# A two-block network on one core: constants loaded behind the first inputs, the feed-forward's first weights split ahead of the last residual, and attention filled by one paced lane

## The chip, the core and the metric

The kernel runs on one core of a Trainium2 chip. The metric is the device time of one execution in microseconds (us), 3388.86 us as the median of three runs before the change. The core's engines each run their own program in order and meet only at semaphores: TensorE (PE, matmuls), VectorE (DVE), ScalarE (ACT), GpSimd (POOL) and SyncE (SP), whose program here issues all DMAs on one queue.

## What is computed

Everything is float32. A first block (a gated linear attention layer and a dilated attention layer, both with memory attention) is followed by a second block of two layers, l = 0 and l = 1. The second block is where most of the change lies. Cut to what matters:

```python
def mixer(hl, hc, ...):                      # 512 latent rows, 256 context rows
    pl, pc = split_projection(hl @ w_in), split_projection(hc @ w_in)
    ... hgrn2_scan forwards and backwards, 4 heads, chunks of 64 ...
    ... diff_softmax_attend: s = q k^T (two maps), p = softmax(s), w = p0 - lam * p1, o = w v
    ... fourier_mix ...
    yl = concat([hgrn, diff, fourier]) @ w_out        # and yc for l = 0

def swiglu(h, w_i, w_o):
    g, u = split(h @ w_i, 2)
    return (silu(g) * u) @ w_o

for l in range(2):
    yl, yc = mixer(...)
    xl = xl + ml[2] * rms_norm(yl, g[1])
    xl = xl + ml[5] * rms_norm(swiglu(adaln(xl, g[2], ml[3], ml[4]), w_ffn_in[l], w_ffn_out[l]), g[3])
    if l == 0: the same for xc
```

The rows are held as tiles of 128: six tiles (four latent, two context) in layer 0, four in layer 1. In the first block, `first_block` begins with `rmsnorm(mem, mem_norm_w)`, which is the first arithmetic of the whole kernel.

## The kernel before

The kernel records one plan: `P.add(kind, ...)` appends a step, and afterwards each engine's program goes through the steps in the order recorded and runs its own handler for each kind. So the order in which the Python code adds steps is the order of the instructions on every engine. No scheduler moves anything; a step that has to wait holds back everything behind it on its engine. Generators (`project`, `prepare`, `levels_early`, `residual_rows`) yield between groups of steps, and `rounds`, `with_some` and `together` decide how two such lanes are mixed: `rounds` takes one step of each in turn, `with_some(a, b, 1.5)` takes one of `a` and then 1.5 of `b`.

**Start.** The step `setup` makes SP issue the loads of `CONST_LOADS` (one of 68 KB and 16 small ones) and then the memory rows `in_mem` (1 MB). Three loads for the gates follow (`w_gate_up`, `k_gla` twice), then the first memory weights (1 MB) and `x`. PE's `setup` transposes the constants. ACT works out the memory rows' norm from a Square, then Ln and Exp; each function set needs a table (`ActQueue.activation` loads one, L169, when the function is not in the loaded set), and the Square is the first of them. All ACT functions have the line L171, and the first table load has it too.

**Attention stage.** `attention_stage` runs the differential attention, tile by tile and four heads per tile. For each head PE makes the scores (L2124), DVE the maxima (L2811) and the weights (L2818 to L2823), PE transposes the weights (L1919) and multiplies them with the values (L1915, 128x64). After a tile's last head DVE finishes with L2832, L2834, L2839. Between the pieces, `fill` takes steps from `filling`: the recurrence's projections `project(0)` and `project(1)`, and the preparation of the recurrence's first head, `prepare(heads[0])` (matmuls of 128x128, DVE L2616) and `levels_early(heads[0])`, the first unit's levels (DVE L2630 x7, one 1792-wide ACT exponential, DVE L2639 x7). What `filling` has left after the last head is recorded behind it, and then comes `fence()`, at which all engines meet. Behind the fence the recurrence begins.

**Output projection.** `project_out` multiplies tile by tile, halves c = 0 and c = 1 of the columns, with weights that were split into a high and a low part (OC0h and OC0l in layer 0, OC1h and OC1l in layer 1). Before a tile's products it records `turned(i + 1)`, the next tile's transposes, whose high part ACT or DVE writes to HI and whose low part DVE writes to LO (L2561). In the middle of each half `between` is called, and after each tile `after_y`. Both take a step of `rows`, which makes the gain rows: DVE L2771 and L2776 build a diagonal in AR, PE multiplies it with a block of ones (`rr`, MATMUL PS<-AR,CON), and ACT or DVE copies it out (L2781). The banks of `rr` are those of the transposes (0 and 1, ring `tr`). `after_y` then adds the residual `rs` (two ACT Squares of 512, DVE L2795, L2800, L2803) and the norm that begins the feed-forward (`norm_begin`: ACT Square, DVE L2482; `norm_end`: eight transposes of HNB, DVE L2494, L2498, and the low part L2504).

**Feed-forward.** Weights arrive by `stage_w` (1 MB each) and `convert` splits a quarter of them: ACT copies the high part to WC (`cvh`, 128x1024), then DVE subtracts to get the low part (`cvl`, L2856). The ring `wcr` has three pieces of WC, which lie over the parts OC. `up` multiplies a quarter (c of 0 to 3) for all tiles; the last tile's rows come later than the others', so the two opening quarters are multiplied first for the columns whose tiles are ready (512 in layer 0, 384 in layer 1), then `norm_end(last)` puts the last tile's transposes, and then the rest of the columns of both quarters (256 and 128 wide). `gated_ff` empties the banks of a block (ACT silu into EX, DVE L2862, ACT high part, DVE L2867), and `up` of the next block's c = 0 waits for all six banks together:

```python
need = [x for i in range(6) for x in ufree.get(i, ())] if c == 0 else []
up_n = up(c, o, [ready, *need], whole)
```

## Time and profile before

| | us |
|---|---|
| median of three runs | 3388.86 |
| lowest and highest | 3388.45, 3390.48 |
| profiled execution, its own time | 3390.33 |
| its span | 3389.0 |
| PE busy in the span | 3026.1 (89%) |
| DVE, ACT, POOL busy | 1578.2 (47%), 989.1 (29%), 325.3 (10%) |

The profile is of one execution. A row gives the start of a group of equal instructions, the time that they took, the engine, the line, the operation with output and input names, the number, and in brackets the idle time before them with what released the engine. PE runs at one of two clocks, 2.4 GHz where the granted clock is 1.00 and 1.2 GHz where it is 0.50; a window's value is the mean over the window.

### The profile page before, as it was taken

To read this page: it belongs to the slowest core of one execution; us is meant where nothing else is said; L and a number is where in the kernel's file an instruction comes from. 1 tells how busy PE (TensorE), PEld (TensorE's weight loads), DVE (VectorE), ACT (ScalarE), POOL (GpSimd) and SP (SyncE) were. 2 spreads that over 40 slices of the span, in tenths; PEclk is the share of its full clock that TensorE was granted. 3 is DMA by queue.
4 is the path that set the end of the run, shared out by engine and by line. 5 is a ranking of instruction groups with operands and counts; after the bars stand their busy time and mean duration, and the time that the engine had idled before them with its cause. 6 is when DMAs were issued, how large, how long until landed. Compare 5 with 4: busy or idle time off the path is not lost.

```text
span 3389.0 us, 44137 instructions
## 1 busy us (share of the span) xinstructions
PE 3026.1 (89%) x18434; PEld 2419.5 (71%) x18434; DVE 1578.2 (47%) x3075; ACT 989.1 (29%) x1913; POOL 325.3 (10%) x594
## 2 busy tenths in 40 slices
PE   6988899999989997887688999999999786789998
PEld 4657588888976566776466888887657676468886
DVE  3122534444442354768662433425535657644444
ACT  2011423232341344334232121212235333222222
POOL 0000000000000000555300000000100334100001
PEclk9999899999999997998798999999999788889999
DMA  5423232222221200323502121121020111123322
GB/s 175 156 97 113 90 111 57 56 57 64 61 107 74 69 13 1 97 76 106 175 18 70 50 75 63 50 75 63 38 62 13 29 28 37 50 71 104 99 87 75
DMA packets 227235, 246.62 MB, mean 73 GB/s; under 512 B 5488, under 2 KB 192988, under 8 KB 225500
## 3 DMA queue, kind: packets, MB, share of 16 engines
q1 hardware_dynamic: 227036, 243.79, 22.4%
q8 instruction: 146, 2.39, 0.3%
q14 instruction: 53, 0.43, 0.0%
HBM read 234.34 MB, written 9.44 MB: 72 GB/s over the span
## 4 chain that ended last, share of the span: by engine, by line
PE 52%; DVE 8%; issue 6%; ACT 3%; POOL 2%; DMA 1%; POOLq 0%; DVEq 0%; ACTq 0%; SPq 0%
PE PS L1915 49%; PE PS L1919 1%; ACT AR L171 1%; PE PS L2124 1%; DVE AR L2639 1%; POOL AR L2916 1%; DVE AR L2875 1%; DVE AR L2630 1%; POOL AR L2907 1%; DVE EX L2862 0%; ACT L169 0%; DVE AC L2867 0%; ACT EX L171 0%; ACT WC L171 0%; DMA WR<-in_w_in 0%
## 5 line engine op out<-in xcount | busy, mean ns | idle before, releaser
L1915 PE MATMUL PS<-HI,WC 128*128 128x512 f32 (+3 forms) x2144 | 581.8, 359 | 30.9 <-DVE EX L2862 12.5
L1915 PE MATMUL PS<-WR,HT 128*128 128x256 f32 (+2 forms) x2256 | 509.9, 384 | 13.3 <-ACT AR L171 7.1
L1915 PEld LDWEIGHTS PS<-WR,HT 128*128 128x128 f32 x2256 | 376.8, 197 | 122.1 <-issue 76.8
L1915 PEld LDWEIGHTS PS<-HI,WC 128*128 128x128 f32 x2144 | 389.7, 194 | 89.3 <-issue 13.1
L1915 PE MATMUL PS<-AR 128*64 128x64 f32 (+8 forms) x3756 | 330.2, 279 | 111.8 <-POOL AR L2916 34.7
L1915 PEld LDWEIGHTS PS<-AR 128*64 128x64 f32 (+5 forms) x3756 | 285.7, 182 | 164.3 <-issue 50.1
L1915 PE MATMUL PS<-LO,WC 128*128 128x512 f32 (+3 forms) x1072 | 384.3, 358 | 0.0
L171 ACT ACTIVATE AR<-PS 128x512 f32<-128x512 f32 (+4 forms) x383 | 164.5, 453 | 670.4 <-PE PS L1915 524.4
L1915 PE MATMUL PS<-HT,WR 128*128 128x256 f32 (+3 forms) x1136 | 348.9, 460 | 10.4 <-DMA WR<-in_w_in 4.6
L1915 PE MATMUL PS<-DW,DH 128*128 128x384 f32 (+1 forms) x1344 | 355.6, 347 | 1.0 <-ACT DH L171 1.0
L2856 DVE TENSOR_TENSOR WC<-WR,WC 128x1024 fp32r<-128x1024 f32 x132 | 161.6, 1225 | 390.6 <-ACT WC L171 390.6
L1915 PE MATMUL PS<-WC,AC 128*128 128x512 f32 x1320 | 318.2, 397 | 11.6 <-DVE AR L2875 9.9
L1915 PEld LDWEIGHTS PS<-WC,AC 128*128 128x128 f32 x1320 | 244.4, 189 | 80.1 <-DVE AR L2875 28.6
L1915 PEld LDWEIGHTS PS<-HT,WR 128*128 128x128 f32 (+2 forms) x1136 | 209.1, 190 | 117.7 <-issue 90.0
L171 ACT ACTIVATE WC<-WR 128x1024 fp32r<-128x1024 f32 x132 | 139.7, 1059 | 512.1 <-PE PS L1915 491.7
L1915 PEld LDWEIGHTS PS<-DW,DH 128*128 128x128 f32 x1344 | 240.8, 191 | 9.7 <-issue 7.1
L1915 PEld LDWEIGHTS PS<-LO,WC 128*128 128x128 f32 x1072 | 208.4, 194 | 27.7
L1915 PE MATMUL PS<-DW,DL 128*128 128x384 f32 (+1 forms) x672 | 226.5, 337 | 0.0
L1919 PE MATMUL PS<-CON,AR 128*128 128x128 f32 (+1 forms) x944 | 156.4, 294 | 71.9 <-ACT AR L171 18.5
L1919 PEld LDWEIGHTS PS<-CON,AR 128*128 128x128 f32 (+1 forms) x944 | 121.2, 151 | 112.8 <-issue 55.4
L171 ACT ACTIVATE EX<-PS 128x256 f32<-128x256 f32 (+2 forms) x158 | 67.6, 431 | 418.8 <-PE PS L1915 418.7
L2875 DVE TENSOR_TENSOR AR<-AR,PS 128x512 f32<-128x512 f32 x200 | 133.6, 682 | 46.1 <-PE PS L1915 46.1
(288 smaller groups left out, 3435.7 us busy)
## 6 DMA issues: line engine op xcount, KB each, us to landing
WR<-in_w_ffn_in SPq DMA_DIRECT2D x44, 1024.0 KB, 7.0
WR<-in_w_in_b SPq DMA_DIRECT2D x51, 512.0 KB, 5.9
WR<-in_w_mod SPq DMA_DIRECT2D x12, 2048.0 KB, 7.9
WR<-in_w_mod SPq DMA_DIRECT2D x24, 1024.0 KB, 5.4
WR<-in_w_ffn_out SPq DMA_DIRECT2D x22, 1024.0 KB, 4.9
WR<-in_w_in SPq DMA_DIRECT2D x40, 512.0 KB, 4.1
WR<-in_w_out SPq DMA_DIRECT2D x8, 2048.0 KB, 8.7
WR<-in_w_in_a SPq DMA_DIRECT2D x8, 1024.0 KB, 5.4
```

Of the source, the lines that this page charges most:

```text
L171: return self.o.activation(out, in_, func, **kw)
L1915: mm = lambda o, l, r, start, stop: e.o.matmul(o, l, r, start=start, stop=stop, skip_group_check=True)
L1919: m = e.o.transpose(bk[0:a.shape[1], 128 * i:128 * i + a.shape[0]], a, ident[0:a.shape[0], 0:a.shape[0]])
L2124: m = e.o.matmul(bank(2 * m_ + b)[:, 0:hi - lo], a.q[m_], a.k[m_][:, lo:hi], start=True, stop=True)
L2630: s = tt(v(x3[:, l, :])[:, :, 0 if rev else 1, :], b4[:, :, 0 if rev else 1, :], ref.broadcast_to([K, 128 // h, h]), ALU.subtract)
L2639: m = tt(v(x3[:, l, :]), v(x3[:, l, :]), v(H.q[:, 128 * i:128 * i + 256]), ALU.mult)
L2856: tt(lo, src, hi.bitcast(F32), ALU.subtract).then_inc(sem("cv_d"))
L2875: tt(y, y, bk, ALU.add).then_inc(sem("dn_d"))
L2907: s = tt(v(x3[:, l, :])[:, :, 1 if rev else 0, :], ref.broadcast_to([K, 128 // h, h]), b4[:, :, 1 if rev else 0, :], ALU.subtract)
L2916: m = tt(v(x3[:, l, :]), v(x3[:, l, :]), v(k[:, 128 * i:128 * i + 256]), ALU.mult)
```

## The change

Three places are rewritten.

At the start a step `begin` precedes everything: SP issues `in_mem` and the 68 KB constant, ACT loads the table of Ln and Exp. Then comes the first load of memory weights, then `setup` with the small constants, then `x`, and only then the three loads for the gates. PE and ACT still wait for all constants in `setup`.

In the output projection of both layers `after_y` no longer takes a step of `rows` at the first tile. For the last tile, the loads of the first feed-forward weights and the split of their first quarter are recorded ahead of `rs`, and each WC piece waits for the products that read the parts beneath it. The last tile's `norm_end` moves between the two opening quarters. `up` waits for each bank where it opens it, in the order 0, 2, 1, 3.

In the attention stage `filling` runs `project(0)`, then `project(1)` with 1.5 steps of preparation and first levels for each of its steps.

```diff
+    def preload(self, func):
...
-        P.add("setup")
+        P.add("begin")
...
         fetch()
+        P.add("setup")
         P.add("inputs")
+        P.add("ld", "gcon", WGU[0:16, :], A["w_gate_up"].rearrange("o a n -> (o a) n"), 0, ())
+        P.add("ld", "gcon", R64, A["k_gla"][:, 0:512].bitcast(F32), 0, ())
+        P.add("ld", "gcon", CAUSAL, A["k_gla"][:, 512:576], 0, ())
...
-            filling = itertools.chain(project(0), rounds([project(1), itertools.chain(prepare(heads[0]), levels_early(heads[0]))]), third_set())
+            first = itertools.chain(prepare(heads[0]), levels_early(heads[0]))
+            filling = itertools.chain(project(0), with_some(project(1), first, 1.5), first, third_set())
...
+            first_tile = 0
+
...
             def after_y(i, ps, bs, GV=GV, rows=rows, xneed=xneed, SQs=SQs, TMs=TMs, items=items, hn=hn, tmps=tmps, HH=HH, cols=cols, cneed=cneed, l=l):
-                next(rows, None)
+                if i != first_tile:
+                    next(rows, None)
                 gneed = [("rr_a", rr_counts["a"]), ("rr_d", rr_counts["d"])]
+                if i == nt - 1:
+                    for j, p in enumerate((ps[0], ps[1], ps[1])):
+                        wcr.until[j] = (("pj", p.n),)
+                    stage_w("up", 0)
+                    stage_w("down", 0)
+                    convert("up", 0, 0)
                 n = P.add("rs", [bank(b) for b in bs], [p.n for p in ps], SQs, TMs, xt(i), GV[:, 0 if i < 4 else 1, :], [*gneed, *xneed])
...
                 if i == nt - 1:
                     v.banks, v.until = (6, 7), (*out_until[6], *out_until[7])
-                    stage_w("up", 0)
-                    stage_w("down", 0)
-                    convert("up", 0, 0)
...
-                return need, lo, hi, [(ubank[q_, s_][1][:, lo - first:hi - first], lo == first and not (s_ == 1 and q_ % 2 == 1)) for q_ in range(4)]
+                return need, lo, hi, [(q_, ubank[q_, s_][1][:, lo - first:hi - first], lo == first and not (s_ == 1 and q_ % 2 == 1),
+                                       tuple(ufree[ubank[q_, s_][0]])) for q_ in (0, 2, 1, 3)]
...
-            free = [x for i in range(6) for x in ufree.get(i, ())]
             for c, (j, o, ready) in enumerate(opening):
-                up(c, o, [ready, *free], [span_of(0, early_tiles, 0, cut)])
-            th = norm_end(items[-1])
+                up(c, o, [ready], [span_of(0, early_tiles, 0, cut)])
+                if c == 0:
+                    th = norm_end(items[-1])
...
-                    need = [x for i in range(6) for x in ufree.get(i, ())] if c == 0 else []
-                    up_n = up(c, o, [ready, *need], whole)
+                    up_n = up(c, o, [ready], [span_of(s_, th, lo, hi) for s_, (lo, hi) in enumerate(fspans)])
...
-                    for q_, (p, opens) in enumerate(places):
+                    for q_, p, opens, free in places:
+                        e.wait_all(free)
...
+            def begin(n):
+                e.preload(ACT.Ln)
...
+            def begin(n):
+                e.o.dma_start(MX, A["mem"].rearrange("o (i p) n -> p (o i) n", p=128)).then_inc(sem("mem"), 16)
+                for to, src in CONST_LOADS[:1]:
+                    e.o.dma_start(to, src).then_inc(sem("const"), 16)
+
             def setup(n):
-                for to, src in CONST_LOADS:
+                for to, src in CONST_LOADS[1:]:
                     e.o.dma_start(to, src).then_inc(sem("const"), 16)
-                e.o.dma_start(MX, A["mem"].rearrange("o (i p) n -> p (o i) n", p=128)).then_inc(sem("mem"), 16)
```

**The first instructions of ACT,** from the start of the program, before:

```order
0 L171 ACT_TABLE_LOAD
1 L171 ACTIVATE EX,STAT<-EX 128x1024
2 L169 ACT_TABLE_LOAD
3 L171 ACTIVATE STAT<-STAT,CON 128x1
4 L171 ACTIVATE STAT<-STAT 128x1
```

and after:

```order
0 L169 ACT_TABLE_LOAD
1 L174 ACTIVATE EX,STAT<-EX 128x1024
2 L174 ACTIVATE STAT<-STAT,CON 128x1
3 L174 ACTIVATE STAT<-STAT 128x1
4 L174 ACTIVATE HNB,STAT<-EX 128x1024
```

One table load is left, and it stands ahead of the wait for the constants.

**DVE at the end of layer 0's attention.** Before, L2839 is the attention's last operation, and the first unit's levels (L2630 seven times, L2639 seven times) begin two rows behind it:

```order
1029 L2832 TENSOR_TENSOR AR<-AR 128x256
1030 L2834 TENSOR_REDUCE STAT<-AR 128x4
1031 L2839 TENSOR_TENSOR AR<-AR,STAT 128x256
1032 L2616 SCALAR_TENSOR_TENSOR AR<-AR,XC,PS 128x128 x2
1033 L2630 TENSOR_TENSOR AR<-EX 128x2x64
1034 L2630 TENSOR_TENSOR AR<-EX 128x4x32
1035 L2630 TENSOR_TENSOR AR<-EX 128x8x16
```

After (L2631, L2645 and L2854 are the changed kernel's lines for L2616, L2630 and L2839), they begin here, between softmax chains,

```order
1009 L2836 TENSOR_SCALAR AR<-AR,STAT,MISC 128x768
1010 L2838 SCALAR_TENSOR_TENSOR AR<-AR,STAT 128x768
1011 L2631 SCALAR_TENSOR_TENSOR AR<-AR,XC,PS 128x128 x2
1012 L2645 TENSOR_TENSOR AR<-EX 128x2x64
1013 L2645 TENSOR_TENSOR AR<-EX 128x4x32
1014 L2645 TENSOR_TENSOR AR<-EX 128x8x16
```

and what follows the attention's last operation is already the next unit, which lies behind the fence:

```order
1043 L2842 COPY AR<-PS 128x64 x2
1044 L2847 TENSOR_TENSOR AR<-AR 128x256
1045 L2849 TENSOR_REDUCE STAT<-AR 128x4
1046 L2854 TENSOR_TENSOR AR<-AR,STAT 128x256
1047 L2645 TENSOR_TENSOR AR<-EX 128x2x64
1048 L2645 TENSOR_TENSOR AR<-EX 128x4x32
```

The first unit's fourteen operations now stand ahead of the last two softmax chains (in layer 1, ahead of and beside the last one).

**PE in tile 1's products of layer 1's output projection,** where AR,CON is a pair of `rr`. Before:

```order
5084 L1915 MATMUL PS<-OC1h_2_235,LO_230 128x512
5085 L1915 MATMUL PS<-OC1h_3_236,HI_229 128x512
5086 L1915 MATMUL PS<-AR,CON 128x512 x2
5087 L1915 MATMUL PS<-OC1l_245,HI_229 128x512
5088 L1915 MATMUL PS<-OC1h_3_236,LO_230 128x512
5089 L1915 MATMUL PS<-OC1h_4_237,HI_229 128x512
```

and after, where the same pair stands:

```order
5103 L1926 MATMUL PS<-OC1h_2_241,LO_230 128x512
5104 L1926 MATMUL PS<-OC1h_3_242,HI_229 128x512
5105 L1926 MATMUL PS<-AR,CON 128x512 x2
5106 L1930 MATMUL PS<-CON,AR 128x128 x8
5107 L1926 MATMUL PS<-OC1l_246,HI_229 128x512
```

The pair has moved from the middle of tile 1's first half to the middle of its second half, 19 rows on, and the fourth pair from there to behind the tile.

## Rows read from the trace of the kernel before

**Rows 1.** Page, busy time: engine, us, share of the span, instructions:

```profile
PE 3026.1 (89%) x18434; PEld 2419.5 (71%) x18434; DVE 1578.2 (47%) x3075; ACT 989.1 (29%) x1913; POOL 325.3 (10%) x594
```

**Rows 2.** Timeline, start, all engines: start us, us, engine line operation xcount [idle before]:

```profile
0.73 0.39 SPq L2935 DMA_DIRECT2D CON<-k_const  x1
...
6.59 0.41 SPq L2936 DMA_DIRECT2D EX<-in_mem  x1
...
7.53 0.90 PE L1919 MATMUL PS<-CON,EX 122*128 122x122 f32 x4 [7.53 <-DMA EX<-in_da_subln]
...
11.70 1.28 ACT L171 ACT_TABLE_LOAD   x1 [11.70 <-DMA EX<-in_mem]
...
14.16 1.28 ACT L169 ACT_TABLE_LOAD   x1
...
16.11 0.75 DVE L2482 TENSOR_SCALAR EX<-EX,STAT 128x1024 f32<-128x1024 f32 x1 [7.05 <-ACT STAT L171]
```

**Rows 3.** DMA issues from 5 to 14 us: KB each, us to landing:

```profile
XC<-in_w_gate_up SPq DMA_DIRECT2D x1, 24.0 KB, 4.8
```

**Rows 4.** Timeline of PE, end of layer 0's attention:

```profile
1314.95 4.53 PE L1915 MATMUL PS<-AR 128*128 128x128 f32 x20 [3.21 <-DVE AR L2616]
...
1336.26 4.00 PE L1915 MATMUL PS<-AR 128*128 128x128 f32 x16
...
1355.45 1.55 PE L1915 MATMUL PS<-AR 128*64 128x64 f32 x24 [9.50 <-POOLq L2888]
```

**Rows 5.** Windows of PE: us, busy (x), granted clock, DMA share, GB/s:

```profile
1313.00:1343.00 30.00, 25.48 (x100) 0.50 0.00 1
```

**Rows 6.** Timeline of DVE, end of layer 0's attention:

```profile
1347.73 0.43 DVE L2839 TENSOR_TENSOR AR<-AR,STAT 128x256 f32<-128x256 f32 x1 [0.60 <-ACT STAT L171]
...
1351.86 3.12 DVE L2639 TENSOR_TENSOR AR<-AR,EX 128x128 f32<-128x128 f32 x7 [1.76 <-ACT AR L171]
```

**Rows 7.** Timeline of PE, end of layer 1's attention:

```profile
2668.73 1.55 PE L1915 MATMUL PS<-AR 128*64 128x64 f32 x24 [9.50 <-POOLq L2888]
```

**Rows 8.** Timeline of PE, layer 0, tile 1 of the output projection:

```profile
1703.63 0.39 PE L1915 MATMUL PS<-OC0h,HI 128*128 128x512 f32 x1
...
1712.48 3.63 PE L1915 MATMUL PS<-AR,CON 128*128 128x512 f32 x4 [8.46 <-DVE LO L2561]
...
1721.83 1.88 PE L1915 MATMUL PS<-AR,CON 128*128 128x512 f32 x4
```

**Rows 9.** Timeline of DVE, the same stretch:

```profile
1704.53 1.29 DVE L2776 TENSOR_TENSOR AR<-CON,MISC 128x512 f32<-128x512 f32 x2
...
1712.25 0.48 DVE L2561 SCALAR_TENSOR_TENSOR LO<-PS,MISC,HI 128x256 fp32r<-128x256 f32 x1
```

**Rows 10.** Timeline of SP and PE, opening of layer 0's feed-forward:

```profile
1773.67 1.01 SPq L2947 DMA_DIRECT2D WR<-in_w_ffn_in  x2
...
1785.68 0.79 PE L1915 MATMUL PS<-HI,WC 128*128 128x512 f32 x1 [5.31 <-DVE WC L2856]
...
1804.06 0.36 PE L1915 MATMUL PS<-HI,WC 128*128 128x256 f32 x1 [3.88 <-DVE LO L2504]
```

**Rows 11.** Page, DMA issues: feed-forward weights, KB each, us to landing:

```profile
WR<-in_w_ffn_in SPq DMA_DIRECT2D x44, 1024.0 KB, 7.0
```

**Rows 12.** Timeline of DVE, the split of the first quarter:

```profile
1784.41 1.22 DVE L2856 TENSOR_TENSOR WC<-WR,WC 128x1024 fp32r<-128x1024 f32 x1
```

**Rows 13.** Windows of PE, the narrow rest, layers 0 and 1:

```profile
1804.00:1811.50 7.50, 7.44 (x49) 0.77 0.00 0
...
3009.60:3020.00 10.40, 10.40 (x49) 0.50 0.15 40
```

**Rows 14.** Timeline of ACT and PE, from the first to the second block:

```profile
1829.53 0.87 ACT L171 ACTIVATE EX<-PS 128x512 f32<-128x512 f32 x2
...
1835.93 0.77 PE L1915 MATMUL PS<-HI,WC 128*128 128x512 f32 x1 [7.72 <-DVE EX L2862]
...
3037.30 0.77 PE L1915 MATMUL PS<-HI,WC 128*128 128x512 f32 x1 [4.76 <-DVE EX L2862]
```

More of the change, by code:

```diff
@@ L164 @@
     loaded = None
-    def activation(self, out, in_, func, **kw):
+    def preload(self, func):
         need = ACT_SET.get(func)
@@ L1846, in build @@
             convert(*work[3])
-            whole = [span_of(s_, th, lo, hi) for s_, (lo, hi) in enumerate(fspans)]
             at_ = 4
@@ L2418, in gt_end @@
                 e.activation(hi, v, ACT.Copy).then_inc(sem("gt_h"))
[L2420 removed]
+            return dict(begin=begin, setup=setup, setup2=setup2, fence=fence, norm1=norm1, norm2=norm2, pj1=pj1, pjc=pjc, ma_x=ma_x, mod_h=mod_h, ga=ga, turn=turn_, gl=gl, hp1=hp1, hp3=hp3,
                         hl1=hl1, ho=ho, g1=g1, g3=g3, g6=g6, qturn=qturn, da_x=da_x, da_t=da_t, fnorm=fnorm, rr=rr, an=an, rs=rs, df_x=df_x, df_t=df_t, df_q=df_q,
@@ L2964, in stored @@
                 e.wait_ge("dump", 16 * P.count["dump"])
-            return dict(setup=setup, inputs=inputs, load=load, ld=ld, dump=dump_, store=store, stored=stored)
+            return dict(begin=begin, setup=setup, inputs=inputs, load=load, ld=ld, dump=dump_, store=store, stored=stored)
         def dumped(e):
```

6 lines of the change are left out of this document (2 added, 4 removed).

## The prediction

> **What bounds the kernel now.** I read the busy times first. TensorE is busy 89% of the span [rows 1], so a change gains only where TensorE stands still or runs at its lower clock. Then I looked up, in the timelines, the four places that the edits touch, and read what released TensorE there. At the start nothing but a chain through ACT and DVE is running [rows 2]. At the end of each attention TensorE waits 9.50 us for POOL's side of the fence [rows 4, 7], and for 30 us before that it ran at a granted clock of 0.50, its 1.2 GHz level [rows 5]. In the output projection it waits 8.46 us for a LO part [rows 8], in the feed-forward's opening 5.31 us for the split and 3.88 us for the last tile's low part [rows 10], and between the first and the second block of weights 7.72 and 4.76 us [rows 14]. In all of these the wait named is TensorE's own, and nothing else covers it. The sum below is made against the profiled execution, 3390.33 us, which is 1.47 above the median of 3388.86.
>
> **Start.** Before, `in_mem` is issued at 6.59 and has landed at 11.70, so it takes 5.1. Its table load of 1.28 follows, then the Square at about 13.0, then a second table load of 1.28 at 14.16, and DVE's first norm operation at 16.11 [rows 2]. The constants' last issue ends about 6.6, and TensorE's setup begins at 7.53, so small constants take 0.9 to land [rows 2]. After, `in_mem` goes first, at 0.73, and lands near 6. The small constants end their issues about 0.85 later than before, since two 0.4 us issues come ahead, which alone would make them land at 8.4. But 2 MB are ahead of them on the queue: 24 KB issued behind `in_mem` took 4.8 to land [rows 3]. I take 9.0 for the constants, with 8.4 to 11.5 as bounds (the upper if each pays what `w_gate_up` paid). The Square then starts at 9.0 and not at 13.0, and the second table load is gone: 4.0 + 1.3 = **5.3 us**, bounds 2.8 and 5.9. The three gate loads are needed much later, and nothing waits for them now.
>
> The Trainium skill ("DMA: Bandwidth & Descriptors", section "Queues, rings and completion order") says that each DMA engine takes descriptors in ring order. That rule speaks against placing small constants, for which two engines wait, behind 2 MB, and the row of 4.8 us agrees with it. By that rule alone the gain is near the lower bound. The skill also gives ("ScalarE: Activation LUTs", section "What ACT_TABLE_LOAD costs") about 2.66 us for a change of table, a drain included. By the page this part would gain 1.4 us more. The rows show 1.28 from one ACT instruction to the next, so the measurement decides for the smaller.
>
> **Attention, layer 0.** After the attention's last DVE operation (1347.73 to 1348.16) come the first unit's levels, ending at 1354.98 with L2639, and TensorE resumes at 1355.45 [rows 4, 6]. The change records these between the last heads' operations, so of the 7.3 us behind L2839 about 0.5 is left for the fence: 6.8 gained. The preparation's matmuls (x20, 4.53 us, and x16, 4.00 us [rows 4]) stood in the stretch at half clock, where TensorE was busy 25.48 of 30 us [rows 5]. They are now spread in front of it, among dense projections at full clock, where they cost half: 4.3 gained. Against this, the levels' DVE work and the 4.6 us of L2630 and L2639 now stand in front of a head's softmax, and an operation that waits holds back DVE in order. I allow 1 us: 6.8 + 4.3 - 1 = **10.1 us**. Bounds 0 (below) and 14, if TensorE keeps its higher clock for part of the remaining heads.
>
> **Attention, layer 1.** The same gap of 9.50 stands there [rows 7], and only the x16 group, since the levels now lie within the last head's own chain and cost some of what they save. 6.8 + 2.0 less a part of the 4.6 us of levels that the chain cannot hide, about 0.8: **8 us**, bounds 0 and 11.6.
>
> **Gain rows.** TensorE stops at 1704.0 in the first half of tile 1 and waits for a bank until DVE's LO is written at 1712.73 [rows 8, 9]. After, it runs on without the pair: 9.35 us lie between the third and the fourth pair [rows 8], of which about 3 are the third pair itself at half clock and the rest is work, 6.4, so that TensorE reaches the new place at 1703.9 + 5.9 = 1709.8, at full clock. DVE does not make the diagonal ahead of the residual any more, which takes 1.4 us [rows 9] off LO's time: 1711.3; then come the diagonals, and the pair can run at 1712.8. So it stands where the fourth stood at 1721.83: 9.0 earlier, and the fourth pair, now behind the tile, costs 1.7. That is **7.3 us**, and as much in layer 1, where the same gap stands: 14.6. Bounds 6 and 8.5 each.
>
> **Opening.** The first weights are issued at 1773.67, the second of the two about 0.5 later, and land 7.0 after [rows 10, 11], near 1781.5. ACT's copy (I take 1.1, a little less than the operation of the same size on DVE) and DVE's low part (1.22 [rows 12]) follow. Before, DVE reached it only after two residual operations, at 1784.41, and TensorE started at 1785.68 [rows 10, 12]. Moved ahead of the residual, the split ends at 1784.1. Only 1.5 is gained, since the load's landing is late next. ACT reads its two Squares behind a copy that waits for this load, so the last residual is 3 us later. That is covered: the transposes now stand behind the first opening quarter. Both quarters took 13.5 us with the transposes' 1.0 taken off (1785.68 to 1800.18 [rows 10]), so each gives 6.7 of cover (5.0 in layer 1, where columns are 384 wide) for a chain of 3.88 from transposes to LO. So the gap of 3.88 goes. So does the low clock that followed it: 0.77 over 7.5 us in layer 0, which is 1.7 us, and 0.50 over 10.4 us in layer 1, 5.2 us [rows 13]. **Layer 0: 1.5 + 3.9 + 1.7 = 7.1; layer 1: 1.5 + 3.9 + 5.2 = 10.6.** Bounds 4 to 8, and 5 to 13. In layer 1 the cover is thinnest, about 1 us; if the clock stays low in the 128-wide rest even without an idle ahead, 5.2 falls away.
>
> **Bank by bank.** ACT begins to empty the first bank at 1829.53, and it is read by about 1830.1; TensorE waits for the last, until 1835.93 [rows 14]. With a wait for each bank, in the order 0, 2, 1, 3, it starts at 1830.15, and each bank comes free before TensorE has done the one ahead: **5.8 us**. In layer 1 only four banks have to be emptied, and I take 2.8 of the wait of 4.76 [rows 14]. Bounds 4 and 6.5; 2 and 4. Later blocks' banks are free early already and gain nothing.
>
> **The sum** is 5.3 + 10.1 + 8.0 + 14.6 + 7.1 + 10.6 + 5.8 + 2.8 = 64.3 us. The profiled execution would take 3326.0, the median 3324.6. That is my forecast, 3324.
>
> **Rivals.**
> - *The pacing gains nothing.* In the filled stretch TensorE is dense, and preparation at 1.5 steps waits there for its own DVE operations (the 3.21 us for L2616 [rows 4] is such a wait), in order, with scores behind it. Then 18 us of attention gain are given back and the rest holds: 46, that is 3342. For it: the row. Against: fewer heads are left bare.
> - *The clock stays low in the narrow rest, and late residuals use up the cover.* Layer 1's opening gives 5 and layer 0's 4, so 9 less in all: 3333. For it: the narrow rest ran at 0.50 throughout [rows 13]. Against: in front of it there would be no idle time.
> - *The constants land late,* at 11.5: 2.5 less, 3326. It is also the answer of the ring-order rule, and lies inside my range.
> - *Slower than before.* One wait like that of 3.21 us in the dense stretch lowers the clock, as the 30 us at 0.50 behind it show [rows 4, 5]. If the interleaved preparation keeps causing such waits, everything in the stretch is at half clock. Work of t us at full clock costs t more. To lose the 46 us of the other parts, 23 us of such work in each layer would have to fall there, behind a gain of 18 that is not made; from there on the kernel is slower. With 30 us in each layer, it gives 3342 + 60 = 3402. Against it: the stretch before ran at full clock even beside steps of the same kind.
> - *The change doesn't do what it says.* The start, the gain rows and the banks are fixed by order alone; if each of the other waits is only replaced by a later one (splits for landing, levels for ACT), 28 is left: 3361.
>
> **How the numbers follow.** I give the forecast with the constants' rival 0.60, the clock rival 0.14, no gain from pacing 0.16, only replaced waits 0.06, slower 0.02, and a gain larger than my upper bounds 0.02. The lower end takes the high bounds in both attentions and in layer 1's opening, 4 + 3.6 + 2.4 above my terms and 3 elsewhere: 3324 - 13 = 3311, rounded to 3310. The upper end has to reach the pacing rival, 3342. A measurement of this kernel can tell about 0.2%, 6.8 us, from no change. Faster by more than that 0.96, within 0.02, slower 0.02.
>
> **What would show it.** Right: `in_mem`'s landing near 6 and DVE's first norm near 10.8; one table load ahead of it; no L2639 of the first unit behind the attention's last operation, and a wait at that fence of below 3 us; no wait above 4 us for LO in tile 1; no wait between the opening quarters and their rest, with clock 1.00 there; TensorE's second block starting within 2 us of ACT's first EX. Wrong: a window at 0.50 that is longer than before ahead of the fences, waits for DVE AR L2631 (L2616 before) among projections, a wait for HNB between the two opening quarters, or first operations that wait for a constant until beyond 11.

## The result, and the profile after

The changed kernel takes 3348.14 us (median of four executions, 3343.95 to 3348.71), the kernel before 3389.67. The ratio is 0.987, with a 95% interval of 0.9859 to 0.9881: 41.5 us faster, where 64 were forecast and 3324 us was the time. 3348.14 lies 6 us outside the range, whose upper end was 3342. The profiled execution, with a span of 3342.6, was the fastest of the four.

The windows view of TensorE, cut where both kernels have put the same matmuls behind them, says where the time went. Layer 1's attention is cut at 2565.0 and 2535.4, ahead of the projections among which the change places the first preparation. Its columns are the stretch, its length, TensorE's busy time (number), the granted clock, DMA share and GB/s. Before:

```profile
7.50:1224.20 1216.70, 1115.01 (x6200) 0.96 0.29 90
1224.20:1356.80 132.60, 113.73 (x554) 0.81 0.00 1
1356.80:1676.20 319.40, 249.81 (x3455) 0.89 0.32 101
1676.20:1732.30 56.10, 43.05 (x132) 0.86 0.28 112
1732.30:1788.40 56.10, 50.79 (x211) 0.96 0.18 57
1788.40:1838.60 50.20, 38.60 (x201) 0.87 0.13 42
1838.60:2565.00 726.40, 706.06 (x3441) 1.00 0.18 60
2565.00:2670.20 105.20, 88.02 (x463) 0.84 0.01 2
2670.20:2925.80 255.60, 193.16 (x1964) 0.84 0.15 47
2925.80:2995.70 69.90, 55.76 (x201) 0.90 0.14 46
2995.70:3039.10 43.40, 34.76 (x151) 0.78 0.15 49
```

and after:

```profile
11.70:1219.80 1208.10, 1113.06 (x6202) 0.96 0.28 89
1219.80:1343.50 123.70, 109.12 (x554) 0.86 0.00 1
1343.50:1662.80 319.30, 254.14 (x3455) 0.89 0.32 101
1662.80:1714.30 51.50, 44.13 (x132) 0.90 0.31 124
1714.30:1768.90 54.60, 50.74 (x212) 0.97 0.18 58
1768.90:1805.70 36.80, 34.74 (x202) 0.99 0.19 58
1805.70:2535.40 729.70, 708.50 (x3442) 0.99 0.18 60
2535.40:2647.50 112.10, 93.07 (x463) 0.83 0.01 2
2647.50:2904.10 256.60, 194.32 (x1965) 0.85 0.15 47
2904.10:2963.90 59.80, 53.28 (x202) 0.97 0.16 53
2963.90:2993.20 29.30, 27.24 (x152) 0.94 0.22 72
```

Row by row against the sum. Both kernels have a second profile each, with spans of 3391.4 and 3350.5, and the table takes both; gains are of the means.

| stretch | forecast | before | after | gained |
|---|---|---|---|---|
| end of the first stretch | 5.3 | 1224.2, 1226.8 | 1219.8, 1224.7 | 3.3 |
| layer 0, attention | 10.1 | 132.6, 132.5 | 123.7, 123.7 | 8.9 |
| layer 0, recurrence | 0 | 319.4, 319.4 | 319.3, 324.5 | -2.5 |
| layer 0, gain rows | 7.3 | 56.1, 55.9 | 51.5, 47.5 | 6.5 |
| layer 0, products up to the split | 1.5 | 56.1, 56.1 | 54.6, 54.7 | 1.4 |
| layer 0, opening and banks | 11.4 | 50.2, 50.3 | 36.8, 38.6 | 12.6 |
| to layer 1's attention | 0 | 726.4, 726.4 | 729.7, 730.1 | -3.5 |
| layer 1, attention | 8.0 | 105.2, 105.2 | 112.1, 112.0 | **-6.9** |
| layer 1, recurrence | 0 | 255.6, 255.7 | 256.6, 256.4 | -0.8 |
| layer 1, gain rows and split | 8.8 | 69.9, 69.9 | 59.8, 60.0 | 10.0 |
| layer 1, opening and banks | 11.9 | 43.4, 43.4 | 29.3, 29.2 | 14.1 |

So the feed-forward's half of the change gave about what was forecast. Layer 1's attention became 6.9 us longer where it should have become 8 shorter, and two stretches that the change does not touch became longer too. Four stretches wander between executions of one program: the end of the first, layer 0's recurrence, its gain rows, and its opening, which took 36.8 us in one profile and 38.6 in the other. Of the recurrence's 2.5 most is such wandering: in fifteen profiles of kernels with the whole of the new feed-forward or all but one part of it, it took 317.7 to 325.2 us, 320.4 in the mean.

The waits at the places of [rows 8, 10, 14], in the timeline of TensorE after:

```profile
1699.80 2.62 PE L1926 MATMUL PS<-AR,CON 128*128 128x512 f32 x4 [2.31 <-DVE AR L2791]
...
1766.16 0.79 PE L1926 MATMUL PS<-HI,WC 128*128 128x512 f32 x1 [3.86 <-DVE WC L2871]
...
1804.15 0.47 PE L1926 MATMUL PS<-HI,WC 128*128 128x512 f32 x1 [2.06 <-ACT EX L174]
```

The wait of 8.46 us for LO has become one of 2.31 for the diagonal (I had 3.0 for it). The one of 5.31 for the split is 3.86, the gap of 3.88 behind the transposes is gone now that they stand in the middle of the opening, and that of 7.72 for the banks is 2.06. In layer 1 the values are 2.30, 3.74 and 2.06.

### The profile page after: what moved, and what is told of

The parts are those of the page before. It is cut to its first block, busy times and chain, and to the rows that moved or that the text cites. A ratio compares the mean times of both kernels' runs of the same rounds, so it can differ in the third digit from the quotient of the medians.

```text
span 3342.6 us, 44104 instructions
## 1 busy us (share of the span) xinstructions
PE 3019.2 (90%) x18434; PEld 2410.6 (72%) x18434; DVE 1578.4 (47%) x3075; ACT 988.3 (30%) x1912; POOL 320.9 (10%) x594
## 4 chain that ended last, share of the span: by engine, by line
PE 55%; DVE 9%; ACT 4%; issue 2%; DMA 1%; POOL 1%; SPq 0%; DVEq 0%; ACTq 0%; POOLq 0%
PE PS L1926 51%; PE PS L1930 2%; DVE AR L2654 1%; PE PS L2135 1%; ACT AR L174 1%; DVE AR L2645 1%; DVE AR L2890 1%; ACT L169 1%; DMA WR<-in_w_in 1%; POOL AR L2931 1%; DMA WR<-in_w_ffn_in 0%; DVE STAT L2826 0%; ACT WC L174 0%; ACT EX L174 0%; DVE EX L2877 0%
## 5 line engine op out<-in xcount | busy, mean ns | idle before, releaser
L1926 PE MATMUL PS<-HI,WC 128*128 128x512 f32 (+3 forms) x2144 | 571.5, 354 | 11.7 <-DVE WC L2871 7.6
L1926 PE MATMUL PS<-WR,HT 128*128 128x256 f32 (+2 forms) x2256 | 518.8, 388 | 16.8 <-ACT AR L174 6.3
L1926 PEld LDWEIGHTS PS<-HI,WC 128*128 128x128 f32 x2144 | 381.8, 190 | 68.7 <-DVE WC L2871 9.3
L174 ACT ACTIVATE AR<-PS 128x384 f32<-128x384 f32 (+4 forms) x383 | 164.7, 454 | 670.3 <-PE PS L1926 526.1
L1926 PE MATMUL PS<-WC,AC 128*128 128x512 f32 x1320 | 317.4, 396 | 11.9 <-DVE AR L2890 10.3
```

The source lines that it names most:

```text
L174: return self.o.activation(out, in_, func, **kw)
L1926: mm = lambda o, l, r, start, stop: e.o.matmul(o, l, r, start=start, stop=stop, skip_group_check=True)
```

## Layer 1's attention: the waits, and what stands behind them

After, the timeline of TensorE in that stretch has these rows, the larger waits among them:

```profile
2582.36 6.71 PE L1926 MATMUL PS<-WR,HT 128*128 128x256 f32 x16 [3.55 <-ACT XC L174]
...
2597.85 3.77 PE L1926 MATMUL PS<-AR 128*128 128x128 f32 x20 [2.98 <-DVE AR L2631]
...
2601.41 5.72 PE L1926 MATMUL PS<-WR,HT 128*128 128x256 f32 x16
...
2614.61 2.00 PE L1926 MATMUL PS<-AR 128*128 128x128 f32 x16 [1.37 <-DVE AR L2631]
...
2646.00 1.55 PE L1926 MATMUL PS<-AR 128*64 128x64 f32 x24 [2.28 <-DVEq L2491]
```

The 9.50 us at the fence [rows 7] have become 2.28. In their place TensorE waits 3.55 us for ACT and 2.98 and 1.37 for DVE's L2631, among the projections. All its waits in the stretch add up to 19.0 us (112.10 less 93.07), before to 17.2. So the waits alone explain 1.8 of the 6.9 us. The rest stands in the windows above: TensorE's busy time in the stretch went from 88.02 to 93.07 us for the same 463 matmuls. The windows view cut finer shows where, before:

```profile
2640.00:2660.00 20.00, 16.93 (x68) 0.50 0.00 1
2660.00:2670.20 10.20, 1.47 (x28) 0.50 0.03 11
```

and after:

```profile
2582.30:2589.00 6.70, 6.64 (x17) 0.54 0.00 0
2597.80:2607.00 9.20, 9.15 (x37) 0.63 0.00 0
2624.00:2647.50 23.50, 15.85 (x84) 0.50 0.02 6
```

Before, the lower clock lay over the last 32 us only, and over the wait at the fence it cost nothing, since TensorE was busy 1.47 of those 10.2 us. After, it lies over the bare heads as before, and also over two pieces of dense projection: the 16 matmuls of 2582.36 take 6.71 us and those of 2601.41 5.72, where the same group takes 3.72 and 3.67 with no wait near it. The two cost 5.1 us more, which is the whole growth of the busy time. The loss repeats: the second profile has 112.0, and five other kernels with 1.5 in layer 1 have 111.5 to 113.7.

**Undone in layer 1 alone, and in both layers.** The edit for layer 1 alone is this; for both layers `rounds([project(1), first])` stands without the condition.

```diff
-            filling = itertools.chain(project(0), with_some(project(1), first, 1.5), first, third_set())
+            filling = itertools.chain(project(0), with_some(project(1), first, 1.5) if both else rounds([project(1), first]), first, third_set())
```

> As the changed kernel, but layer 1's attention is filled as before the change (projection and preparation in turn, one step each, levels behind the attention); layer 0 keeps the new pacing. Theory: the new pacing costs 6 to 7 us in layer 1, because TensorE waits 3.55 us for ACT and 2.98 us for DVE among the projections and loses its higher clock twice; then this kernel is 5 to 8 us faster than the changed one, near 3341. Rival: the loss there comes from the clock's luck, and this kernel is within 2 us of the changed one or slower, since the 7 us of levels come back behind the attention.

> As the changed kernel, but both layers' attentions are filled as before. Theory (new pacing gains 8 us in layer 0 and costs 6 to 7 in layer 1, as the two traces put side by side read): within 2 us of the changed kernel, 3346 to 3350, and about 8 us slower than the kernel in which layer 1 alone is filled as before. The rival that pacing gains in both layers gives 3358 to 3366.

Measured: 3340.51 us (3337.70 to 3346.03) with layer 1 as before, and 3349.88 (3347.45 to 3352.87) with both, beside 3348.31 for the changed kernel. So by the medians the new pacing costs 7.8 us in layer 1 and gains 9.4 in layer 0, near what the windows gave (6.9 and 8.9). With the old filling layer 1's stretch is 106.0 and 106.1 us long in these two kernels, 6 us shorter than with the new. So the loss in layer 1 is the pacing's.

**What the wait for ACT is.** In the changed kernel ACT's timeline shows three table loads of 1.28 us around the gates' sigmoids and the query's Silu, and the copies of the preparation's bank (XC) behind them:

```profile
2572.41 1.28 ACT L169 ACT_TABLE_LOAD   x1
...
2576.77 1.28 ACT L169 ACT_TABLE_LOAD   x1
...
2578.71 1.28 ACT L169 ACT_TABLE_LOAD   x1
...
2581.77 0.44 ACT L174 ACTIVATE XC<-PS 128x128 f32<-128x128 f32 x2
```

Before, the same three loads (2600.99 to 2608.57) were followed by a wait of 1.23 us only, since two groups of projection, 7.4 us of TensorE's time, lay between. A kernel without these loads, in which the gate and the query lose their sigmoid and Silu:

```diff
-                e.activation(kf, lg, ACT.Sigmoid, scale=-1.0).then_inc(sem("hg_s"))
-                e.activation(lg, lg, ACT.Sigmoid).then_inc(sem("hg_s"))
+                e.activation(kf, lg, ACT.Exp, scale=0.0).then_inc(sem("hg_s"))
+                e.activation(lg, lg, ACT.Exp, scale=0.0).then_inc(sem("hg_s"))
...
-                e.activation(q, q, ACT.Silu).then_inc(sem("hq"))
+                e.activation(q, q, ACT.Copy).then_inc(sem("hq"))
```

> As the changed kernel, but the recurrence's gates are an exponential of zero in place of a sigmoid, and its queries a copy in place of Silu, so that ACT changes no table there; the gate's and query's values are left out by this. It takes away 3 table loads of 1.28 us in the stretch in which layer 1's TensorE waits 3.55 us for ACT XC. Theory (ACT, held by 3.84 us of table loads between attention exponentials, empties the preparation's bank late): that wait is gone (under 0.5 us), and with it the run at 0.50 behind it, which took 6.71 us for 16 matmuls instead of 3.7. Rival (the wait comes from another engine's work, ACT is only last): 2 us or more of it stay, with another releaser.

The timeline of TensorE without the loads, the same place:

```profile
2578.89 1.45 PE L1926 MATMUL PS<-AR 128*128 128x64 f32 x12
2580.17 3.67 PE L1926 MATMUL PS<-WR,HT 128*128 128x256 f32 x16
...
2592.63 4.02 PE L1926 MATMUL PS<-AR 128*128 128x128 f32 x20 [2.99 <-DVE AR L2631]
```

The wait for ACT is gone, and the group behind it takes 3.67 us. The wait for DVE's L2631 stays at 2.99. So the first wait is ACT's tables, as the theory had it. The second is another matter: six gate operations and two copies stand ahead of L2631 in DVE's order, and the 20 matmuls of the preparation that need it follow with only one group of projection in between; that is read from the two timelines, and no run took the gate operations away. The kernel took 3335.09 us in its one execution, but it saves table loads in other places too, so the total is not the price of the wait. Its own stretch is: 105.4 us and not 112.1. These 6.7 us are close to the sum of the wait of 3.55 and the 3.0 that the slow group behind it costs, and they are nearly the whole loss against the kernel before (105.2).

**Is it the pace or the place?** Three kernels change only the number 1.5, in layer 1 to 1.2, 2 and 3; one has 2 in both layers.

> As the changed kernel, but in layer 1 the preparation takes 1.2 steps for each projection step and not 1.5; layer 0 keeps 1.5. With 1.2 the preparation's transposes and 128x128 matmuls fall later among the projections, and there are as few bare heads at the end as with 1.5. Theory A (what costs time in layer 1 is where the first preparation group falls against ACT's three table loads and sigmoids, 1.5 only happens to be a bad place): this kernel has no wait of over 3 us for ACT XC and is 6 to 12 us faster than the changed one, 3336 to 3342. Theory B (levels and preparation within the attention cost what they cost, whatever the pace): 3345 to 3350, as the changed one.

> As the changed kernel, but in layer 1 the preparation takes 2 steps for each projection step, so that it comes still earlier. Theory A (an accident of place) allows any time from 3336 to 3352; the number and place of waits of over 2 us in front of the last two heads must explain it. Theory B (the earlier the preparation the more often TensorE waits for its operands among the projections): 3350 to 3358, slower than the changed kernel.

> As the changed kernel, but in layer 1 the preparation takes 3 steps for each projection step. Theory B (earlier is better): 3332 to 3337. Theory A (place decides): anything from 3334 to 3350, with the sum of waits and the time at 0.50 in the stretch from the first projection to the fence explaining the difference to the kernel with 2.

> As the changed kernel, but the preparation takes 2 steps for each projection step in both layers. With layer 1 alone at 2 it took 3336.6. Theory A (what decides is the place at which preparation falls against ACT's table loads and DVE's gate operations, which differs between the layers): layer 0 can win or lose up to 8 us, 3330 to 3345, and the trace must show other waits there than those of 1.04, 3.20 and 2.13 us. Theory B (earlier is better, since operands of the last groups are ready): 3331 to 3336.

| steps in layer 1 (layer 0) | time, us | layer 1's stretch | its large waits |
|---|---|---|---|
| 1, as before (1.5) | 3340.51 | 106.0 | 1.25 ACT, 3.34 DVE, 9.50 fence |
| 1.2 (1.5) | 3342.27 | 106.1 | 5.29 ACT, 1.23 DVE, 3.63 fence |
| 1.5 (1.5), the change | 3348.14 | 112.1 | 3.55 ACT, 2.98 and 1.37 DVE, 2.28 fence |
| 2 (1.5) | 3336.59 | 104.4 | 3.55 ACT, 2.92 DVE, 2.28 fence |
| 3 (1.5) | 3341.08 | 106.2 | 5.81 DVE, 2.28 fence |
| 2 (2) | 3340.21 | 104.4 | as with 2 |

By their medians all other paces are 6 to 12 us faster than 1.5, so the theory that levels and preparation within the attention cost what they cost in any mixture fell, and so did the one that with 2 the kernel would be slower than with 1.5. With 1.2 my forecast of no wait of over 3 us for ACT was wrong: there is one of 5.29, and the stretch is short all the same. So the size of the first wait does not decide. With 2 it is the same 3.55, and the stretch is 7.7 us shorter. The timeline of TensorE with 2:

```profile
2586.56 6.00 PE L1926 MATMUL PS<-WR,HT 128*128 128x256 f32 x16 [3.55 <-ACT XC L174]
...
2599.93 3.67 PE L1926 MATMUL PS<-WR,HT 128*128 128x256 f32 x16
...
2613.92 0.85 PE L1930 MATMUL PS<-CON,AR 128*128 128x128 f32 x6 [2.92 <-DVE AR L2842]
```

DVE's gate operations stand ahead of L2631 here too (2597.32 to 2600.83, then L2631 at 2602.72), but no matmul comes so early that it would wait for it. The projections behind run in 3.67 us and not in 5.72. One wait of 2.92 comes when the projections are over, and the bare heads behind it wait 0.41 us each for DVE, where those of the changed kernel wait 1.18, 1.72 and 1.43. All waits are 12.8 us and not 19.0, and the busy time is 91.6 and not 93.1 for the same 463 matmuls. That accounts for the 7.7 us. In layer 0 the same step from 1.5 to 2 changes the waits (1.19 and 0.41 us where 3.20 and 2.13 stood) and not the length (123.3 against 123.7). That "earlier is better" fell as well: with 3 the stretch is 1.8 us longer than with 2, 3.3 more of waits and 1.5 less of busy time. What is left, beside the table loads that a run has shown, is where the groups come to stand in TensorE's row against ACT's table loads and DVE's gate operations; that is a reading of these six timelines, and no run moved a single group to show it.

Timed again, the kernel with 2 in layer 1:

> The changed kernel with 2 steps of preparation for each projection step in layer 1, once more, nothing else edited. It took 3336.6 (3335.7 to 3336.9); with the small constants moved as well it took 3340.5 (3333.4 to 3343.6). Theory: 3335 to 3341, that is 7 to 13 us faster than the changed kernel and not clearly different from the filling of before in layer 1 (3340.5). Rival (its first timing was a lucky chip or moment): 3341 or more.

3339.16 us (3337.63 to 3343.31), beside 3336.59 the first time; the ratios to the kernel before are 0.9841 (0.9825 to 0.9858) and 0.9834 (0.9819 to 0.9848). By the medians that is 9 to 12 us faster than the change. It is the fastest version that was timed in several rounds. By its total it is not told apart from the old filling of layer 1 (0.9842, 0.9826 to 0.9859); by its own stretch it is 1.6 us shorter (104.4 in each of three profiles, against 106.0 and 106.1).

## The start

> The kernel before with the change's start alone (memory rows and the 68 KB constant issued first, one table load ahead of the wait, small constants behind the first memory weights, gate loads behind x). The two traces show DVE's first norm operation at 13.49 and not 16.11, and TensorE's first memory-weight product 2.6 us earlier, with a faster clock over it in the one trace of the changed kernel. Theory: 2.6 us faster than the kernel before, plus or minus what the clock does, 3386 to 3389. Rival (the 4.4 us by which the changed kernel's trace is ahead at 420 us all come from the start): 4 to 5 us faster.

The timeline of the changed kernel, ACT's Square and DVE's first norm operation, and TensorE's first memory product:

```profile
11.66 1.06 ACT L174 ACTIVATE EX<-EX 128x1024 f32<-128x1024 f32 x1 [9.64 <-DMA EX<-in_da_subln]
...
13.49 0.75 DVE L2497 TENSOR_SCALAR EX<-EX,STAT 128x1024 f32<-128x1024 f32 x1 [0.28 <-ACT STAT L174]
...
20.20 3.69 PE L1926 MATMUL PS<-HT,WR 128*128 128x256 f32 x16 [2.23 <-DVE HT L2509]
```

The constants landed at 11.66, just beyond the upper bound that I had given (11.5), and the norm comes 2.6 us earlier than at 16.11 [rows 2], not 5.3. By the Trainium skill ("DMA: Bandwidth & Descriptors", "Queues, rings and completion order") descriptors are taken in ring order. The trace agrees: by that rule I had put the gain near the lower bound of 2.8, and the constants landed behind the 2 MB. The start alone took 3390.76 us (ten executions) beside 3391.69, with an interval of the ratio of 0.9988 to 1.0007: between 4.1 us faster and 2.4 slower. Its median is above the 3386 to 3389 that I had expected, and the interval holds 2.6 as well as nothing, but not 5.3. The end of the first stretch tells more, since nothing else of the change lies ahead of it: 1224.2 and 1226.7 us in the two profiles of the kernel before, 1222.4 in the mean of fourteen profiles with this start (1219.8 to 1224.9). So about 3 us had arrived there.

> As the changed kernel, but the 16 small constants are issued ahead of the first memory weights, so that 1 MB and not 2 MB lies in front of them. In the changed kernel ACT and PE waited for them until 11.66. Theory (the queue's order holds them back): they land near 8.7 to 9.3, ACT's Square starts there, and the first norm operation of DVE comes 2.4 to 3 us earlier; of that 1 to 3 us arrive at the end of the kernel (memory weights land 6 us later than now, which is still before they are needed). Rival (issue, not transfer, sets the time: the last small one is issued at 7.99 now and would be at 7.5): 0.5 us earlier only.

```diff
-        fetch()
         P.add("setup")
+        fetch()
```

ACT's two Squares and the first memory product, in the timeline of this kernel:

```profile
8.59 1.06 ACT L174 ACTIVATE EX<-EX 128x1024 f32<-128x1024 f32 x1 [6.57 <-DMA EX<-in_da_subln]
...
15.38 1.06 ACT L174 ACTIVATE EX<-X 128x1024 f32<-128x1024 f32 x1 [3.47 <-DMA X<-in_x]
...
19.22 6.15 PE L1926 MATMUL PS<-HT,WR 128*128 128x256 f32 x16 [4.71 <-DVE HT L2509]
```

So the mechanism is as expected: with 1 MB less ahead the constants land at 8.59 and the first norm operation of DVE comes 3.1 us earlier (10.41). But ACT then waits 3.47 us for `x`, whose 2 MB come behind the memory weights, and the first product gains only 1.0 us. At the end nothing arrived that these times can tell, 3349.87 us; the rival (0.5 us earlier only) fell, since the landing moved by 3.07 us. Together with the pace of 2 in layer 1:

> The changed kernel with 2 steps of preparation for each projection step in layer 1 and the small constants ahead of the first memory weights. The first alone gave 3336.6, the second alone 3349.9 beside the changed kernel's 3348.3, although it brings the first norm 3.1 us earlier. Theory (the early start is given back, for the memory weights and the clock): 3335 to 3339, the same as with the pace alone. Rival: 3333 to 3335, if the 3 us arrive.

3340.53 us (3333.39 to 3343.60), a little above the 3335 to 3339 of the theory, so this is not better than the pace alone.

## The feed-forward's parts, one by one

> As the changed kernel, but the first tile takes its step of the gain rows again, so the third pair stands in the first half of tile 1. Theory: a wait of 8.4 us for LO comes back in both layers, and the kernel is 13 to 17 us slower than the changed one, 3361 to 3366. Rival (the last residual or the opening is late by something else, so the pair's place matters less): under 10 us.

```diff
-            first_tile = 0
+            first_tile = -1
```

The timeline of TensorE with the pair back, in layer 0 (in layer 1 the wait is 8.44):

```profile
1703.10 3.75 PE L1926 MATMUL PS<-AR,CON 128*128 128x512 f32 x4 [8.45 <-DVE LO L2576]
```

3360.92 us, 12.8 more than the changed kernel (in my sum 14.6), so the rival of under 10 fell.

> As the changed kernel, but the last tile's transposes stand behind both opening quarters again, as before the change. Theory (my sum: 3.9 us of waiting in each layer and the low clock behind it, 1.7 and 5.2): 12 to 16 us slower than the changed kernel, 3360 to 3364. Rival (the clock in the narrow rest is low anyway, only the waits come back): 7 to 9 us, 3355 to 3357.

```diff
-                if c == 0:
-                    th = norm_end(items[-1])
+            th = norm_end(items[-1])
```

With the transposes back behind both opening quarters, the timeline of TensorE in both layers:

```profile
1785.03 0.36 PE L1925 MATMUL PS<-HI,WC 128*128 128x256 f32 x1 [3.88 <-DVE LO L2518]
...
2981.28 0.45 PE L1925 MATMUL PS<-HI,WC 128*128 128x128 f32 x1 [3.88 <-DVE LO L2518]
```

3358.14 us, 10.0 more. The gap of 3.88 is back in both layers, and the narrow rest behind it runs slowly, so the opening with its banks takes 43.6 us in layer 0 and 40.0 in layer 1. In layer 1 it took 29.3, so this is 10.7, and my 9.1 was a little small. In layer 0 it took 36.8 in the changed kernel's first profile and 38.6 in its second, so this is 6.8 or 5.0, around my 5.6. The two come to 15.7 or 17.5, and the kernel shows 10.0, between the theory (12 to 16) and the rival (7 to 9). The stretch between the layers gives 3.3 us back (726.5 against 729.8); the other 2 to 4 are not found in one place, and medians of four differ by as much.

> As the changed kernel, but the second and later blocks' first quarter waits for all six banks together again (the order 0, 2, 1, 3 stays). Theory: TensorE waits some 7 us again in layer 0 and 4 to 5 in layer 1 for DVE's last product; 8 to 11 us slower than the changed kernel, 3356 to 3359. Rival (most of what the traces put on the banks is the higher clock of the stretch behind, which luck gives or takes): under 6 us.

```diff
-                    up_n = up(c, o, [ready], ...
+                    need = [x for i in range(6) for x in ufree.get(i, ())] if c == 0 else []
+                    up_n = up(c, o, [ready, *need], ...
```

With one wait for all banks, the timeline of TensorE in layer 0 (in layer 1 the wait is 4.77):

```profile
1814.35 0.76 PE L1927 MATMUL PS<-HI,WC 128*128 128x512 f32 x1 [7.73 <-DVE EX L2878]
```

3357.89 us, 9.8 more (in my sum 8.6), as the theory had it.

> As the changed kernel, but the loads of the first feed-forward weights and the split of their first quarter stand behind the last residual again. The trace of the changed kernel shows the split's wait at 3.86 us in layer 0 and 3.74 in layer 1, where it was 5.31 in both. Theory (1.5 us in each layer, as summed, with the last residual's 3 us delay hidden): 2 to 5 us slower than the changed kernel, 3350 to 3353. Rival (the last residual, no longer behind ACT's copy, brings the transposes' data earlier and something waits less): 0 to 1 us.

The wait is 5.31 again in both layers, and the stretches ahead of it are 1.4 and 1.6 us longer. All the same the kernel took 3345.80 us (3341.55 to 3348.93), 2.3 less than the changed kernel. My theory (2 to 5 us slower) holds for the place and falls for the kernel; the rival (0 to 1) can't be told from what was measured, since the two ratios, 0.9859 and 0.9869, have intervals that overlap. In the profile the 3 us are given back: the stretch between the layers takes 727.1 us and not 729.8.

## What wanders without any edit

> The changed kernel once more, nothing edited. Its four executions lay between 3343.95 and 3348.71 us, and the profiled one was the fastest. If that spread comes from where the stretches at a granted clock of 0.50 fall (theory: luck of the clock), a second profile shows the same waits in the same places to 0.1 us, while the time at 0.50 (353 us in the first profile) differs by some 4 to 8 us, and the span with it by about half. Rival: some wait is itself different from execution to execution, then the same place shows another idle time.

> The kernel before, nothing edited, for a second profile. Its first profile had 405 us at a granted clock of 0.50, the eleven kernels of this study 353 to 387. Theory (the clock's luck works on both alike): the waits stand where they stood, to 0.1 us, and the untouched stretch from the second block's start in layer 0 (1838.6) to layer 1's projections (2582.4), 743.8 us in the first profile, comes out 1 to 5 us different. Rival (the 2.3 us by which that stretch is longer in the changed kernel are the change's): it is again 743.8 within 0.5.

The changed kernel's second profile has the same waits (3.55, 2.99, 1.37, 2.29 in layer 1's attention), but a span 7.9 us longer and, by the clock records within the span, 375.0 us at 1.2 GHz, where the first had 351.4 (the 353 of the expectation runs 1.5 us beyond the last instruction). That is 24 us and not 4 to 8, and the span moved by a third of it and not by half. The first place where they part is TensorE's first memory product, at 20.20 us in the first profile (above, 3.69 us) and in the timeline of the second:

```profile
20.29 6.70 PE L1926 MATMUL PS<-HT,WR 128*128 128x256 f32 x16 [2.23 <-DVE HT L2509]
```

The wait in front of it is 2.23 us in both. It is not what makes the difference: eight transposes that stand ahead of the wait, and eight of the same size behind the product, show the clock on either side of it. The first profile, in the timeline of TensorE:

```profile
14.30 1.97 PE L1930 MATMUL PS<-CON,EX 128*128 128x128 f32 x8 [1.71 <-DVE EX L2497]
...
23.73 1.04 PE L1930 MATMUL PS<-CON,EX 128*128 128x128 f32 x8
```

and the second:

```profile
14.39 1.97 PE L1930 MATMUL PS<-CON,EX 128*128 128x128 f32 x8 [1.72 <-DVE EX L2497]
...
26.83 1.04 PE L1930 MATMUL PS<-CON,EX 128*128 128x128 f32 x8
```

Ahead of the wait they take 1.97 us in both profiles, behind the product 1.04. So TensorE is at its lower level before the wait, and what differs is when the clock first rises: the trace's first record of a clock of 1.00 begins at 18.2 us in the first profile, ahead of the product, and at 26.4 in the second, when the product is nearly over. With a wait of 2.23 or 2.24 the same 16 matmuls take 5.39 and 6.55 us in the two profiles of the kernel before (first rise at 26.3 and 28.7, product from 22.8), and 5.22 in that of the start alone (23.5, product from 20.4). So one and the same order of work, with the same waits, meets the rise of the clock at another place in each execution.

The stretch from layer 0's second block to layer 1's projections is not of this kind. To 2582.4 it took 743.8 and 743.9 us in the two profiles of the kernel before, so the rival was right. Cut at 2565.0, ahead of all new pacing, it took 726.4, 726.4 and 726.6 us in three profiles of kernels with the old feed-forward, 729.7 and 730.1 in the changed kernel, and 729.8 to 730.8 in nine further profiles with the new feed-forward. So some 3.5 us belong to the change, though none of its edits is there. They lie in two places, where layer 0 ends (38.6 us before, 40.3 and 40.1 after) and 160 us later (17.5 and 19.2). At the first the group of 16 matmuls behind a wait of 2.05 us takes 8.45 and 8.14 us in the changed kernel's two profiles, 7.03 in both of before. With the split or the transposes moved back, both places have the old lengths of 38.6 and 17.5; with the gain rows moved back, only the second has. The change moves the time at which these waits come, and with it how much of the work behind them runs slowly. Why a shift of a few microseconds is enough wasn't tried.

## Why the prediction was wrong

- **Layer 1's attention: the step that failed.** I wrote "6.8 + 2.0 less a part of the 4.6 us of levels that the chain cannot hide, about 0.8: 8 us". It was -6.9, outside my bounds of 0 and 11.6. The first two terms came: the wait at the fence went from 9.50 to 2.28 us (7.2), and the 16 matmuls from 3.99 to 2.00. The step that failed is the cost of 0.8 for the moved work, which was 16.1. The other waits grew by 9.0 us, from 7.7 to 16.7, and the lower clock over the work behind them and in front of the fence cost the other 7.1, 5.1 of it in two groups of projection. I had priced the moved work at DVE's duration, and did not go through the projections to see behind which operation of ACT and DVE each moved group would stand. That is 14.9 of the 22.8 us that are missing. The lower bound of 0 had no reason: a step put into dense work can cost more than it saved where it stood, since it takes the clock with it.
- **The rivals.** "The pacing gains nothing" named the mechanism, but put it at a loss of all 18 us in both layers (3342), and the 3.21 us wait as its pattern. Layer 0 kept its gain of 8.9, and layer 1 lost. The measured 3348 lies beyond this rival's 3342 as well. Two of my signs of being wrong came true: waits for DVE AR L2631 among projections, and first operations that wait for a constant until beyond 11.
- **The start: mis-sized.** 9.0 for the constants' landing was a guess between issue and queue; the queue decides, 11.66. The term is 2.6, not 5.3. The upper bound of 11.5 did not follow from its own row either: issues that end near 7.45 and 4.8 us to landing give 12.2.
- **Untouched stretches: missing from the sum.** The recurrence of layer 0, -2.5 in the mean of two profiles that differ by 5, most of it wandering, and the stretch between the layers, -3.5, which repeats. The sum had no term and the range no allowance for them.
- **Right:** layer 0's attention (10.1 for 8.9), the gain rows (14.6 for 12.8 at the end of the kernel), the opening with its banks (11.4 and 11.9 for 12.6 and 14.1, where layer 0's would be 11.6 by the second profile alone), the banks alone (8.6 for 9.8), the residual's 3 us delay hidden by the first quarter. The clock rival for the narrow rest did not come: in layer 1 the granted clock is 1.00 over the rest (2973 to 2978), and the rest takes 5.3 us where it took 10.4. One step of the gain rows' sum was not worked out: 6.4 us of work are found and 5.9 added; it moves the term by half a microsecond.
- **The split:** 1.5 each at its place, as summed, and nothing at the end.

## What to carry to other kernels

When work is moved from a bare end into dense work, follow each moved group to the instructions that stand ahead of its operands on the other engines, table loads among them; the wait removed at the end is only one side. A wait among dense matmuls can cost nearly its own length once more, since what follows runs at the lower clock (3.0 us behind the wait of 3.55; without the table loads both went), so a pace should be tried at several values: here 1, 1.2, 2 and 3 all beat 1.5. A change of 3 us in a kernel of 3350 is read from the length of its own stretch, not from the total, which wanders by as much. Such a stretch has to be cut where both kernels have put the same matmuls behind them; cut 17 us later, within the reordered work, this one would have shown 7.9 us and not 6.9.

## What the runs showed of the hardware

At the start of the kernel TensorE is at its lower level, 1.2 GHz, and the first record of the higher one came between 18.2 and 28.7 us in five profiles of three kernels; 16 matmuls of 256 columns at that place, behind an idle time of 2.23 us that is the same to 0.01, took from 3.69 to 6.70 us. Later, behind a wait of 2.05 us, the same 16 matmuls of 512 columns took 7.03, 8.14 or 8.45 us, and behind one of 3.55 us 16 of 256 columns took 6.71 or 6.00. Total time at 1.2 GHz differed between executions of one kernel by 24 us (351.4 and 375.0), and the span by 7.9. I had taken a wait's effect on the clock as fixed by its length.
